# Second feed-forward of a two-block transformer layer: strips turned by transposing DMAs, two changed k pairs in place of three

## What is computed

```python
def conv_ffn(h, w_ffn_in, conv_w, conv_b, w_ffn_out):      # D_FF_2 = 5632
    S = h.shape[1]
    up = h @ w_ffn_in                                       # 2048 x 11264
    a, b = up[..., :D_FF_2], up[..., D_FF_2:]
    a_pad = jnp.pad(a, ((0, 0), (CONV_W - 1, 0), (0, 0)))
    a = (conv_w[0] * a_pad[:, 0:S] + conv_w[1] * a_pad[:, 1:S + 1]
         + conv_w[2] * a_pad[:, 2:S + 2] + conv_b)
    return (jax.nn.gelu(a, approximate=True) * b) @ w_ffn_out
```

## Time and profile before

| | us |
|---|---|
| median of 3 runs | 2414.37 (2414.29 to 2414.64) |
| profiled execution | 2415.28 |
| its span in the trace | 2413.5 |
| PE busy | 2400.3 |
| DVE busy | 1880.4 |
| ACT busy | 1449.1 |
| POOL busy | 50.9 |

### The profile page before, as it was taken

How to read it: one execution, slowest core, us unless ns; L and a number is a source line. 1 busy time by engine, 2 the same in 40 slices (tenths; PEclk the granted TensorE clock), 3 DMA queues, 4 the chain that set the end, 5 groups by cost and what they waited for, 6 DMA issues and landing times.

```text
span 2413.5 us, 28853 instructions
## 1 busy us (share of the span) xinstructions
PE 2400.3 (99%) x10993; PEld 1993.1 (83%) x10993; DVE 1880.4 (78%) x2411; ACT 1449.1 (60%) x1798; POOL 50.9 (2%) x93
## 2 busy tenths in 40 slices
PE   9999999999999999999999999999999999999998
PEld 7888888888888888888888888888788888888887
DVE  6455555688889898989777587665789999999877
ACT  6457566445656566666555465664666666666554
POOL 1000110000000000000002000000000000000000
PEclk9999999999999999999999999999999999999999
DMA  7666566656687877777566545655566666666665
GB/s 238 193 182 181 186 171 180 219 189 192 193 218 215 220 217 213 212 209 213 186 212 202 165 148 163 180 191 186 181 197 189 199 198 189 196 192 192 201 215 169
DMA packets 280644, 470.08 MB, mean 195 GB/s; under 512 B 57926, under 2 KB 60144, under 8 KB 279872
## 3 DMA queue, kind: packets, MB, share of 16 engines
q1 hardware_dynamic: 279104, 462.62, 64.4%
q0 software_dynamic: 1376, 5.69, 0.7%
q10 hardware_dynamic: 32, 0.01, 0.0%
HBM read 456.19 MB, written 2.10 MB: 190 GB/s over the span
## 4 chain that ended last, share of the span: by engine, by line
PE 98%; DVE 1%; DMA 0%; SPq 0%; issue 0%; ACT 0%; DVEq 0%; ACTq 0%
PE acc L1075 16%; PE acc L1077 16%; PE acc L1076 16%; PE acc L791 11%; PE acc L793 11%; PE acc L792 11%; PE mis L1077 3%; PE mis L1075 3%; PE mis L1076 3%; PE mis L1354 1%; PE mis L889 1%; PE mis L764 1%; PE mis L1263 1%; PE acc L810 1%; PE acc L811 1%; PE acc L812 1%
## 5 line engine op out<-in xcount | busy, mean ns | idle before, releaser
L1694 ACT ACTIVATE wf<-wf_raw 128x1024 fp32r<-128x1024 f32 x544 | 565.0, 1056 | 495.7 <-DVE wf_raw L2541 205.3
L2553 DVE TENSOR_TENSOR wf<-wf_raw,wf 128x1024 fp32r<-128x1024 f32 x544 | 643.9, 1219 | 75.5 <-ACT wf L1694 71.4
L2209 DVE TENSOR_TENSOR lo<-raw,hi 128x1024 fp32r<-128x1024 f32 (+1 forms) x313 | 376.3, 1219 | 247.2 <-ACT hi L1418 245.0
L1418 ACT ACTIVATE hi<-raw 128x1024 fp32r<-128x1024 f32 (+1 forms) x313 | 320.4, 1048 | 161.5 <-PE acc L793 136.2
L1075 PE MATMUL acc<-wf,xb_hi 128*128 128x512 f32 x931 | 364.4, 391 | 0.0
L1077 PE MATMUL acc<-wf,xb_lo 128*128 128x512 f32 x931 | 362.6, 389 | 0.0
L1076 PE MATMUL acc<-wf,xb_hi 128*128 128x512 f32 x931 | 362.2, 389 | 0.0
L791 PE MATMUL acc<-hi,xa_hi 128*128 128x512 f32 (+1 forms) x576 | 223.9, 389 | 0.0
L793 PE MATMUL acc<-hi,xa_lo 128*128 128x512 f32 (+1 forms) x576 | 221.8, 385 | 0.0
L792 PE MATMUL acc<-lo,xa_hi 128*128 128x512 f32 (+1 forms) x576 | 221.6, 385 | 0.0
L791 PE MATMUL acc<-hi,xb_hi 128*128 128x512 f32 x544 | 216.2, 397 | 0.0
(11 more groups left out here) (537 smaller groups left out, 3831.7 us busy)
## 6 DMA issues: line engine op xcount, KB each, us to landing
raw<-in_w_in SPq DMA_DIRECT2D x215, 512.0 KB, 4.4
wf_raw<-in_w_ffn_in SPq DMA_DIRECT2D x160, 512.0 KB, 3.7
wf_raw<-in_w_gate SPq DMA_DIRECT2D x88, 512.0 KB, 3.8
wf_raw<-in_w_up SPq DMA_DIRECT2D x88, 512.0 KB, 4.1
wf_raw<-in_w_down SPq DMA_DIRECT2D x88, 512.0 KB, 4.5
wf_raw<-in_w_ffn_out SPq DMA_DIRECT2D x88, 512.0 KB, 3.8
wf_raw<-in_w_out SPq DMA_DIRECT2D x32, 512.0 KB, 4.4
raw<-in_w_o SPq DMA_DIRECT2D x32, 512.0 KB, 4.6
```

Source lines behind the costliest of these rows:

```text
L1418: nc.scalar.activation(hi[:, slot, :, 0:width], raw[:, slot, :, 0:width], ACT.Copy)\
L1694: nc.scalar.activation(wf[:, f_slot[c], 0, :, :], wf_raw[:, f_slot[c], 1, :, :], ACT.Copy)\
L2209: V.tensor_tensor(lo[:, slot, :, 0:width], raw[:, slot, :, 0:width], hi[:, slot, :, 0:width].bitcast(F32), ALU.subtract).then_inc(lo_ready, 1)
L2553: V.tensor_tensor(wf[:, f_slot[c], 1, :, :], wf_raw[:, f_slot[c], 1, :, :], wf[:, f_slot[c], 0, :, :].bitcast(F32), ALU.subtract).then_inc ...
```

## The change

- The changed k pairs of the second feed-forward are 0 and 4, where they were 0, 3 and 5 (pair 1: only 4, where it was 3 and 5).
- Strips 0 to 9 are no longer turned by PE. ACT copies a and b into two sets of 16-bit planes (`plane_copy2`, four copies of 1024 half words a pair), SP issues eight transposing DMAs a pair (`turn_plane2`), and ACT joins the halves (`joined`, two copies each for a and b). Only strip 10 is turned by PE, now at k pair 3 of `e0` and not 2.
- SP's DMAs stand among the loads: two behind (7,1), one behind each of (0,0), (0,1), (1,0), (1,1), (2,0), (2,1) of the next pair. Each waits until both planes of its strip are written.
- ACT joins the b strip and scales the next strips between the hi parts of (5,0) and (5,1); the four plane copies stand between (5,1) and (7,1); joining of the a strip comes behind (2,0) of the next pair. `scaled` was behind (2,1) before.
- In the last k pair DVE writes the lo part of (7,0) and (7,1) behind `middle` and `middle_end`, and all four sums of the next k pair 0 follow in one go.
- `finish_up` of a wide pair is one sum 1024 wide in place of two of 512.

```diff
-S_K = dict(out=(0, 3, 5), ffn=(0, 2, 4), ffn2=(0, 3, 5))
+S_K = dict(out=(0, 3, 5), ffn=(0, 2, 4), ffn2=(0, 4))
...
+            def turn_plane2(m, j, h, t):
+                sp.wait_ge(planes2_ok[j], 2 * m + 2)
+                sp.dma_start(tplanes2[j][:, h, :, t * P:(t + 1) * P], planes2[j][:, h, t, :], transpose=True)\
+                    .then_inc(planes2_turned[j], 16)
+
+            def beside_chunk2(p, k, h):
+                if p.stage == "ffn2" and (k, h) == (7, 1):
+                    turn_plane2(p.i - 1, 0, 0, 0)
+                    turn_plane2(p.i - 1, 0, 0, 1)
+                m = FT - 2 if p is e0 else p.i - 2
+                if p.run and p is not e1 and m >= 0 and k == 0:
+                    turn_plane2(m, 0, 1, h)
+                at = ((1, 0), (1, 1), (2, 0), (2, 1))
+                if p.run and p is not e1 and m >= 0 and (k, h) in at:
+                    turn_plane2(m, 1, at.index((k, h)) // 2, at.index((k, h)) % 2)
...
-                    between = None
-                    if p.wide and k == p.nk - 1:
-                        pe.wait_ge(x_ok, p.no + 1)
-                        turn_half(p.i - 1, 0)
-                        between = turn_b
-                    if p is e0 and k == 2:
-                        pe.wait_ge(a_in, FT - 1)
+                    if p is e0 and k == 3:
+                        pe.wait_ge(p1_out, e0.no)
+                        pe.wait_ge(x_ok, e0.no)
                         turn_half(FT - 1, 0)
...
+            def plane_copy2(m, j, h):
+                act.wait_ge(staged, stages(PH["ffn2"][2] + m) - 1 + j)
+                nc.scalar.activation(planes2[j][:, h, :, :], halves_of((stg, stg2)[j][:, :, :])[h], ACT.Copy)\
+                    .then_inc(planes2_ok[j], 1)
+
+            def joined(m, j):
+                act.wait_ge(planes2_turned[j], 64 * (m + 1))
+                act.wait_ge(ff_out, FT + m)
+                for h in range(2):
+                    last = nc.scalar.activation(halves_of((a_sb, b_sb)[j][:, :, :])[h], tplanes2[j][:, h, :, :], ACT.Copy)
+                last.then_inc((a_in, b_in)[j], 1)
...
                 f_hi_of(p, 2, 1)
+                f_hi_of(p, 3, 0)
+                f_hi_of(p, 3, 1)
                 if p.i > F_FIRST:
                     tap(p.i - 2)
+                f_hi_of(p, 4, 0)
+                f_hi_of(p, 4, 1)
+                t_hi_of(p, 4)
+                f_hi_of(p, 5, 0)
+                if p.i > F_FIRST:
+                    joined(p.i - 2, 1)
                     scaled(run_c[p.i - F_FIRST - 1])
...
+                f_hi_of(p, 5, 1)
+                plane_copy2(p.i - 1, 0, 0)
+                f_hi_of(p, 6, 0)
+                plane_copy2(p.i - 1, 0, 1)
+                plane_copy2(p.i - 1, 1, 0)
+                f_hi_of(p, 6, 1)
+                p1_copy(p)
                 if p.i > F_FIRST:
                     gelu(p.i - 2)
...
+                f_hi_of(p, 7, 0)
+                plane_copy2(p.i - 1, 1, 1)
+                f_hi_of(p, 7, 1)
...
+                if p.wide:
+                    V.tensor_tensor(out[:, :, :], acc[1 - p.par][:, :, :], us[:, :, :], ALU.add).then_inc(tile_sum, 2)
+                    return
```

More of the change, by code:

```diff
@@ L241, in two_blocks @@
         ff_raw = at("ff_raw", A0, [KF, T])
+        planes2 = [at(f"planes2_{j}", A0 + (KF - 8 + 4 * j) * T, [2, TT, W], U16) for j in range(2)]
         ff_lo = at("ff_in_place_lo", A0, [KF, T], F32R)
@@ L397, in two_blocks @@
         planes_ok, planes_turned = sem("planes_ok"), sem("planes_turned")
+        planes2_ok = [sem(f"planes2_ok{j}") for j in range(2)]
+        planes2_turned = [sem(f"planes2_turned{j}") for j in range(2)]
         tile_sum, gate_ok, ff_out = sem("tile_sum"), sem("gate_ok"), sem("ff_out")
@@ L1094, in touch @@
                         pe.wait_ge(tile_sum, 4 * p.no)
-                turned_out = 0 if not p.run else FT if not p.wide else p.i - F_FIRST
+                turned_out = FT if p.run and not p.wide else 0
                 if name == "p1" and p in (out0, f1):
@@ L2140, in _ @@
                 f_hi_of(after, 2, 0)
+                joined(p.i - 1, 0)
             for k in range(2, e0.nk):
@@ L3129, in _ @@
                 f_lo_of(p, 2, 0)
+                f_lo_of(p, 2, 1)
+                f_lo_of(p, 3, 0)
+                f_lo_of(p, 3, 1)
+                strassen(p, 4)
                 if p.i > F_FIRST:
                     taps(p.i - 2, 1)
[L3132 removed]
+                f_lo_of(p, 5, 0)
                 if p.i > F_FIRST:
                     taps(p.i - 2, 2)
[L3135 to L3137 removed]
+                f_lo_of(p, 5, 1)
+                f_lo_of(p, 6, 0)
+                f_lo_of(p, 6, 1)
+                middle(p)
+                middle_end(p)
+                f_lo_of(p, 7, 0)
                 if p.i > F_FIRST:
                     gated_conv(p.i - 2)
[L3140 to L3144 removed]
+                f_lo_of(p, 7, 1)
                 after = run_c[p.i - F_FIRST + 1]
                 if after.wide:
[L3147 to L3150 removed]
+                    for _ in sums(after, 0):
+                        pass
                     dve.wait_ge(t4_ok, after.set(0) + 1)
```

81 lines of the change are left out of this document (28 added, 53 removed).

## The result

| | before | after |
|---|---|---|
| median, us | 2414.83 (2414.14 to 2417.72, 12 runs) | 2420.67 (2417.87 to 2422.58, 12 runs) |
| profiled execution | 2415.28 | 2418.66 |
| its span | 2413.5 | 2417.0 |

The ratio is 1.0021, with a 95% interval of 1.0013 to 1.0029: **5.8 us slower**, where 13.1 were forecast. Sign and range held, the size did not. The profiled execution is one of the shorter ones of its twelve, so the traces have only 3.5 us to explain. That the changed kernel itself varies more than the kernel before becomes a finding further down.

What follows compares the result with a forecast made beforehand. The prediction took PE as the bound, busy 2400.3 of 2413.5 us. PE's net -10.4 us and stalls of +23.5 us (8 x 2.9) summed to +13.1, a median of 2427.5 us, range 2407 to 2437.

Steps and rivals of the forecast that it cites:

- e0: First pair of the down projection, behind pair 10; the prediction gave it a plain k pair 0 needing no sums, no stall.
- PE's terms, -10.4 us: Ten pairs of the second feed-forward: turning matmuls removed, 17.2 us; one product more a pair, 6.8 us; net -10.4.
- The wait and its place: SP waits about 3.6 us for ACT's plane copies before the first transposes; PE then stalls at k pair 0, pairs 3 to 10.
- How late the load is: Load (0,1) of the next pair, behind the held transposes in SP's queue, is issued 1.4 us late.
- The landing: Time load (0,1) takes to land among transposes: 6.5 us taken, forecast band 5.5 to 7.2, giving a stall of 2.9 a pair.
- the trio of the earlier trace: In the kernel before, three loads with three transposes in 6 us, landing in 4.6, 5.8 and 6.7 us.
- the looser train of the earlier trace: In the kernel before, loads and transposes in turn, some 2.2 us apart, landing in 5.2 us.
- The last sums: The previous pair's last sums, queued on DVE behind the late difference, cost PE 0.3 us more a pair.
- (5,1): Possible other wait: ACT splits this chunk after joining and scaling, at 15.0; DVE's part to 16.3, PE needs it at 18.4.
- about even: Rival: loads beside transposes land in 4.9 us, stall 1.3 a pair, change 0.0, 2414.4 us; chance 0.20.
- Faster: Rival: loads overtake transposes, load (0,1) lands in 3.9 us, stall 0.3; 2406.6 us, or 2404; chance 0.15.
- Slower still: Rival: queue builds up, load (0,1) lands in 7.5 to 8 us, stall 3.9 to 4.4; 2435 to 2439 us; chance 0.20.

Runs made afterwards that it cites:

- early plane copies: Changed kernel with the a strip scaled and both its plane copies made between ACT's hi parts of (4,0) and (4,1); alone 2407.64 us.
- changed kernel, group 2: The changed kernel, nothing edited, measured again beside the second group of follow-up kernels: 2414.85 us.
- changed kernel, group 3: The changed kernel, nothing edited, measured a third time beside the third group of follow-up kernels: 2414.87 us.
- second a copy later: Changed kernel with the second plane copy of a moved from behind ACT's hi part of (6,0) to behind that of (6,1): 2433.42 us.
- both mends: Changed kernel with a's scaling and plane copies between hi parts (4,0) and (4,1), and the order in `e0` altered on ACT and DVE: 2402.78 us, repeated 2402.49.
- the k pairs alone: Kernel before with changed k pairs 0 and 4 in place of 0, 3 and 5, strips still turned by PE: 2422.16 us.
- the transposes behind the load: Changed kernel with SP issuing all four transposes of a behind load (0,1), plane copies left late: 2411.87 us.
- first run with three k pairs: Changed kernel with a's copies early and `e0` reordered, plus k pairs 0, 3 and 5 changed again in the second feed-forward: 2446.0 us.
- the second, which waits more: As the first run with three k pairs, but ACT's hi parts of the sums stand ahead of scaling, plane copies and joining b: 2455.22 us.

## Why the prediction was right in its mechanism and wrong in its size

The chain from load (0,1) to PE is rigid, so each trace can be read as one sum: the load's issue (counted from the issue of load (4,1)), its landing, and 6.82 us for DVE up to PE's third product; PE would take it at 33.13 us, as it does in every pair of the runs with early plane copies. Means over pairs 3 to 10, worked out from the timelines of SP, DVE and PE:

```
                          load (0,1)          due   PE     stall   last    period
                          issued    lands in        takes          sums
forecast                  22.5      6.5       33.1  35.7   2.6     0.3     45.1
changed kernel, at first  21.99     5.47      33.13 34.28  1.15    0.43    43.70
changed kernel, group 2   21.94     5.03      33.13 33.79  0.66    0.42    43.20
changed kernel, group 3   22.04     5.02      33.13 33.88  0.75    0.43    43.29
second a copy later       23.79     5.10      33.13 35.72  2.59    0.42    45.13
both mends                21.08     3.88      33.13 33.13  0       0       42.16
```

Point by point:

- **PE's terms, -10.4 us.** Confirmed. Turning was taken at 1.72 us a pair; the period without stalls is 42.16, so it costs 43.30 + 0.68 - 42.16 = 1.82. Dropping the k pair cost 7.2 in all against 6.8. The kernel with both mends, in which nothing waits, is 12 us under the kernel before, 1.6 more than the sum had.
- **The wait and its place.** Confirmed: SP at the first transposes for 3.6 us, PE at k pair 0 eight times from pair 3 on, pair 2 in time, the planes ready 17.7 us behind PE's end on (1,1) where 18.0 were worked out.
- **How late the load is.** 1.4 us forecast, 0.9 measured. The three steps to it were each long by a little: planes 17.7 and not 18.0, two transposes in 2.55 and not 2.75, a load and a transpose in 1.86 and not 1.93. Eight times, 0.5 us is 4 us.
- **The landing, the step that failed.** 6.5 us was taken, near the worst of the trio of the earlier trace rows, on the argument that more transposes stand around this load than in that trio. Measured were 5.5, 5.0 and 5.0 us, close to the looser train of the earlier trace rows (4.6 to 5.3) that the text had named and set aside. Eight times 1.0 us is 8 us. The argument counted DMAs in the queue and did not ask whether they were still moving: behind the wait of 3.6 us only load (7,1) of the pair before is still under way, for another 0.5 to 1.3 us, so the first two transposes of a land in 2.4 and 2.5 us (with early copies in 5.5 and 4.9) and are gone 0.7 us before load (0,1) is issued. That their landing early is the reason for 5.5 in place of 6.5 is argued and not shown: no run has a late load with the two still moving.
- **What the standing does to the landing, overlooked.** Against a load that is issued on time it does not help but costs. Load (0,1) goes out 1.86 us behind load (0,0) and not 2.72, so that one needs another 1.9 to 2.5 us to land, against 0.8 to 1.3 in seven of the eight pairs with both mends, and load (0,1) lands in 5.0 to 5.5 us and not in 3.9. On time it has 33.13 - 21.08 - 3.88 - 6.82 = 1.35 us to spare. The 0.9 us of late issue would fit into that; with 1.6 us of longer landing on top they give the stall of 1.15.
- **The last sums.** 0.3 us forecast, 0.43 measured; the width has no part in it.
- **The stall in `e0`, left out.** 2.5 us at first, 1.9 in groups 2 and 3. The prediction walked the wide loop and named (5,1) as the other place at risk, where nothing waited. It did not walk ACT's queue through `e0`, where the change had put the joining of b, and scaling, tap and gelu behind it.

The measured terms together: -12.7 us (the spans of the two traces with both mends, 2400.9 and 2400.6, against 2413.5), +12.3 for the stalls (8 x 1.54) and +2.5 in `e0` are +2.1, where the profiled spans differ by +3.5. Of the missing 1.4 us, 0.6 to 0.9 lie ahead of the first stall: in pair 2 the third product starts at 1781.38 in the changed kernel and at 1780.79 and 1780.43 with both mends. Another 0.4 are the last sums behind the third product of pair 10, which the eight periods don't hold. The forecast in the same terms was -10.4 and +23.5.

As to the rivals: "about even" with a landing of 4.9 us is what groups 2 and 3 ran (2414.9 us, landing 5.0), though by another sum: less lateness, more off PE, and `e0`. "Faster" needed a landing under 4.3 us, which came only where the load was on time. "Slower still" needed 7.5 us or more, and load (0,1) never took longer than 6.0 in the changed kernel. One rule that the prediction had set aside is to be weighed again. The Trainium skill, "Advanced Engine Details and Errata", section X-Bar Transpose (TRN2), says that transposing DMAs are as fast as regular ones. The prediction made 4.9 us of it for the landing of the load beside them, which was nearer to these runs (5.0 to 5.5) than 6.5; for the DMA time that they take these runs do not agree with it, as the last section shows.

What stays open is why load (0,1) landed in 5.5 us at first, where the five later traces with the same queue have 5.0 to 5.1 us, in three groups on three chips. Load (0,0) ahead of it took longer too, 4.2 us on average against 3.9 in groups 2 and 3, so it was not this load alone. One trace can't tell a chip from a moment. And of the 5.8 us between the medians of the changed kernel (2420.67 and 2414.85), the traces of the first measurement and of group 2 have 4.4 in their spans: 4.0 in the eight periods and 0.4 ahead of them (the third product of pair 2 starts at 1781.38 and at 1780.99). The stall of `e0` is 0.6 us shorter in group 2, but there PE loses 0.6 us more at its first product with the strip.

## What to carry to other kernels

Where a queue stands for an engine, ask what the standing does to the DMAs behind it. Here it delayed the issue of the load that counts by 0.9 us, let the transposes ahead of it land early, and sent it out closer behind its neighbour, so that it took 1.1 to 1.6 us longer to land; the late issue alone would have stayed within the 1.35 us of slack. An order that puts a producer on an engine with room (ACT, 62% busy) still costs, if it stands ahead of a DMA queue through which the bounding engine is fed: 1.85 us in its order were 15 in the wide loop, and moving the scaling and two copies forward, with a mend behind the loop, turned a change that won nothing into one that wins 12 us. And when an edit removes the slack of a hand-over that ends in a DMA's landing, measure the kernel more than once, on more than one chip: it had 2420.7, 2414.9 and 2414.9 us with the same code, where the kernel before and the one with both mends repeated within 0.3 us.

## What the runs showed of the hardware

**A stall can take the clock with it.** In the run with early plane copies alone PE stood for 2.7 us in `e0`. The granted clock (the last column but two) of the stretch behind it, then the same stretch of the changed kernel's first trace, whose stall was 2.5 us:

```profile
2189.00:2191.00 2.00, 0.17 (x1) 0.00 (x0) 1.93 (x4) 1.64 (x2) 0.00 (x0) 1.00 0.43 136
2191.00:2193.00 2.00, 1.30 (x3) 1.11 (x4) 2.00 (x3) 2.00 (x3) 0.00 (x0) 0.70 0.56 202
2193.00:2195.00 2.00, 2.00 (x6) 1.52 (x5) 2.00 (x2) 2.00 (x4) 0.00 (x0) 0.50 0.04 8
2195.00:2197.00 2.00, 2.00 (x9) 1.62 (x9) 1.96 (x3) 2.00 (x4) 0.00 (x0) 0.95 0.55 142
```

```profile
2201.00:2203.00 2.00, 0.32 (x2) 0.00 (x0) 1.93 (x3) 1.71 (x2) 0.00 (x0) 1.00 0.49 138
2203.00:2205.00 2.00, 1.37 (x6) 1.15 (x7) 2.00 (x3) 2.00 (x3) 0.00 (x0) 1.00 0.67 232
2205.00:2207.00 2.00, 2.00 (x10) 1.51 (x9) 2.00 (x2) 2.00 (x4) 0.00 (x0) 1.00 0.22 38
```

Behind the longer stall the clock is granted at 0.50, its lower level of 1.2 GHz, and the next eight matmuls start 0.43 us apart in place of 0.227: 1.7 us more. Behind the shorter one it stays at 1.00. So this one stall cost 4.4 us and not 2.7, which is most of the 4.9 us by which both mends stand under the one. Behind the stalls of 2.7 us in the run with the second copy later and in the one with the transposes behind the load, seven or eight matmuls were slow as well. The length of a stall doesn't settle it alone: in the first run with three k pairs, matmuls were slow behind stalls of 2.54, 2.56, 2.65 and 3.16 us, and not behind others of 2.53, 2.66, 2.82 and 3.03 us; in the second, which waits more, also behind one of 2.17 us.

**Transposing DMAs are dear in DMA time, cheap for a neighbour with room around it.** In a pair of the kernel with both mends the DMA engines are busy for 0.84 of 42.16 us, 35.4 us; with the k pairs alone, and no transposes, for 0.60 of 43.98, 26.4 us. Eight transposes of 128 KB are 9.0 us, 1.1 each, as the prediction had from the first feed-forward (1.2). At a load's rate (1.73 us for 512 KB, by the prediction's working) 128 KB would be 0.43. Yet loads (0,1) between two of them, 2.7 us behind the load before, land in 3.7 to 4.4 us with both mends (4.6 at most with early copies alone), where they take 3.6 to 3.7 with none near ahead, in the run with the transposes behind the load. At 1.86 us behind it they take 5.0 to 5.5 on average. No run separates the spacing from the transposes.
